# Gated delta rule: the inverse kept on the other half of the partitions, and copies done by ScalarE

## The chip, the cores and the metric

The kernel runs on one core of one Trainium2 chip. The metric is the device time of one launch in microseconds (us). The kernel before took 1951.79 us (median of 3 runs, 1951.33 to 1960.3).

## What is computed

Two blocks of a network follow each other. The change touches one part of the second: the gated delta rule, over 512 positions, 4 heads of width 128, in both directions. The reference works in chunks of 64 positions:

```python
g = jnp.cumsum(g.reshape(b, h, n, c), axis=-1)
decay = jnp.exp(jnp.where(incl, g[..., :, None] - g[..., None, :], -jnp.inf))
kb = k * beta[..., None]
lower = jnp.where(strict, jnp.einsum('bhnid,bhnjd->bhnij', kb, k) * decay, 0.0)
tmat = lower + jnp.eye(c, dtype=jnp.float32)
rhs = jnp.concatenate([v * beta[..., None], kb * jnp.exp(g)[..., None]], axis=-1)
sol = lax.linalg.triangular_solve(tmat, rhs, left_side=True, lower=True, unit_diagonal=True)
...
def step(state, inp):
    v_new = u_i - jnp.einsum('bhck,bhkv->bhcv', w_i, state)
    o_i = jnp.einsum('bhck,bhkv->bhcv', qg_i, state) + jnp.einsum('bhij,bhjv->bhiv', qk_i, v_new)
    state = state * gl_i[..., None, None] + jnp.einsum('bhck,bhcv->bhkv', kg_i, v_new)
```

The other parts (projections, attention, cross attention, feed-forward, and the whole first block) are the same in both kernels.

## The kernel before

Each engine has its own program, and counting semaphores order them. Nothing plans the order around the change: it is the order in which the loops are written out. The gated delta rule runs in four stages, one after the other; the profile's lines are given in brackets.

**Chunks.** The kernel takes chunks of 128 positions (four, `DN_CHUNKS`), so that the unit-triangular matrix of a chunk is 128x128 for each of 4 heads and 2 directions. For each chunk TensorE (PE) makes decay sums and the products of keys and queries [L2262, `four`], ScalarE (ACT) takes absolute values and exponentials [L1048, L1055, L1056, L1058], VectorE (DVE) builds `dn_lower` [L1553] and the query products [L1556] out of them. PE also turns k and v by token [L2282, L2284], and VectorE copies the turned tiles out of PSUM [L1558, L1559]; PE needs these two banks free for the next chunk (`dn_tok`).

**Inverses.** The inverse of each 128x128 matrix is built from its two 64x64 diagonal blocks. Block 0 lies in partitions 0 to 63, block 1 in 64 to 127 (`HALF`). A group `p` holds 8 matrices, 512 columns; there are 4 groups, and 6 levels, so 24 steps `q = 4 l + p`. A step has two PE calls and two DVE parts:

- `half_products(q)` [L2303]: for 8 matrices and both halves, `dn_lower` times the transposed inverse `dn_inv_t`; 16 products of 64x64.
- `half_masked(q)` [L1574]: DVE multiplies the bank by a mask into `dn_half`. At level 0 it also writes `dn_inv_t` as identity less `dn_half` [L1579], in two instructions, one for each half of the partitions.
- `inverse_products(q)`: from level 1 on, two products for each half, one for `dn_inv_t` [L2324] and one for `dn_inv` [L2327], with 32 moving columns each. At level 0 it turns `dn_half` [L2320].
- `inverse_update(q)`: DVE subtracts both from the inverses [L1593, L1594]; at level 0 it writes `dn_inv` as identity less the turned bank, again in two instructions [L1590].

PE runs `half_products(q)` and then `inverse_products(q - 1)`; DVE runs `half_masked(q)` and then `inverse_update(q - 1)`. Every product of these steps reads partitions of one half and writes PSUM partitions of the same half: it uses the corner (0,0) or (1,1) of the array, where a corner (r,c) is the 64x64 quarter that reads half r and writes half c.

**Corners.** The off-diagonal 64x64 block is made by two more rounds of products [L2343, L2351]. DVE (`corners`) then multiplies the near block by beta [L1605] and the far block by beta [L1606], alternating. Meanwhile GpSimd (POOL) does the same for the other half [L612].

**Recurrence.** Four steps of `v_new`, state and output, in both directions [L2262, L2365, L2385 on PE, L1633, L1639 and others on DVE, L1070 on ACT].

**Small products elsewhere.** The first block also has calls of fp32 products with a 64x64 stationary operand. `scores` [L1892, 32 moving columns] goes in turn through the corners (0,0), (1,0), (0,1), (1,1), and `updates` [L1870, 64 moving columns] through (0,0), (0,1), (1,0), (1,1); in both, what reads half 0 writes one PSUM bank and what reads half 1 another. `carried` [L1917, 64 moving columns] takes only (0,0) and (1,1), into one bank.

A product in fp32 appears in the trace as two records of LDWEIGHTS and two of MATMUL, so a call of 16 products has 32.

Of the kernel before, what the change touches and what calls it, by code (L numbers as in the profile page):

```python
# [22 lines left out]
P = 128  # L23
# [72 lines left out]
def table(entries):  # L96

    at, out = 0, {}
    for name, n in entries:
# [7 lines left out]
CONST2_COLS, N_CONST2 = table([("tri0", P), ("tri1", P), ("inv0", (LEVELS - 1) * HD), ("inv1", (LEVELS - 1) * HD),  # L107
                               ("window", 3 * P), ("rot_half", P), ("inv_freq", 1)])
PAR_COLS, N_PAR = table([("c", 2 * KT), ("norm_g", DEPTH * KT), ("b_mod", DEPTH * N_MOD), ("conv_w", DEPTH * 6),
# [33 lines left out]
def build(nc, tokens, mem, positions, weights, const_d, const2_d, par_d, out):  # L143
    with ExitStack() as ctx:
# [260 lines left out]
        def q_grow(d, c):  # L405
# [52 lines left out]
        dn_grown, dn_qg, dn_qk_ready = sem("dn_grown"), sem("dn_qg"), sem("dn_qk_ready")  # L458
        dn_y_ps, dn_y, dn_z_ps, dn_t = (sem(n) for n in ("dn_y_ps", "dn_y", "dn_z_ps", "dn_t"))
        dn_p_ps, dn_p, dn_c_ps, dn_c, dn_r = (sem(n) for n in ("dn_p_ps", "dn_p", "dn_c_ps", "dn_c", "dn_r"))  # L460
        dn_ks_ps, dn_rhs_ready, dn_v_ps, dn_v, dn_v_end, dn_s_ps, dn_s, dn_o_ps, dn_o = (
# [165 lines left out]
        def _(act):  # L627
# [500 lines left out]
        def _(dve):  # L1128
# [415 lines left out]
            def lower_and_products(n, c):  # L1544

                for d in range(2):
# [9 lines left out]
                    dve.tensor_tensor(dn_qk(u), kq, e, ALU.mult).then_inc(dn_x, 1)  # L1556
                dve.wait_ge(dn_tok_ps, n + 1)
                dve.tensor_copy(k_tok_2(c), by_head(dn_bank(6)))  # L1558
                dve.tensor_copy(v_tok_2(c), by_head(dn_bank(7))).then_inc(dn_tok, 1)  # L1559

            ident_8 = [cst["ident"][rows, rows].unsqueeze(1).broadcast_to([HD, 8, HD]) for rows in HALF]

            def half_masked(q):
# [8 lines left out]
                if 2 <= q < 6:  # L1572
                    dve.wait_ge(dn_t, q - 1)
                dve.tensor_tensor(to_8(dn_half(p)), to_8(dn_bank(p % 2)), mask, ALU.mult).then_inc(dn_y, 1)  # L1574
                if l == 0:
                    dve.wait_ge(dn_y, q + 1)
                    dve.wait_ge(dn_qg, DN_GROWN[NLAT - 1])
                    for r, rows in enumerate(HALF):
                        dve.tensor_tensor(to_8(dn_inv_t(p))[rows], ident_8[r], to_8(dn_half(p))[rows], ALU.subtract)  # L1579

            def inverse_update(q):

                l, p = divmod(q, 4)
                d = p % 2
                side = 1 - d
                dve.wait_ge(dn_z_ps, q + 1)
                if l == 0:
                    to_8 = lambda v: v.rearrange("p (n t) -> p n t", t=HD)
                    for r, rows in enumerate(HALF):
                        ins = dve.tensor_tensor(to_8(dn_inv(p))[rows], ident_8[r], to_8(dn_bank(4 + p % 2))[rows], ALU.subtract)  # L1590
                else:
                    mine, other_side = (lambda v: halves(v, 1 << l)[:, :, side, :]), (lambda v: halves(v, 1 << l)[:, :, 1 - side, :])
                    dve.tensor_tensor(mine(dn_inv_t(p)), mine(dn_inv_t(p)), mine(dn_bank(2 + p % 2)), ALU.subtract)  # L1593
                    ins = dve.tensor_tensor(other_side(dn_inv(p)), other_side(dn_inv(p)), other_side(dn_bank(4 + p % 2)), ALU.subtract)  # L1594
                ins.then_inc(dn_t, 1)

            def corners(n):

                dve.wait_ge(dn_c_ps, n + 1)
                for s in (2 * n, 2 * n + 1):  # L1600
                    for d in range(2):
                        u, c = dn_unit(d, s), chunk_at(d, s)
                        lo, to = HALF[0], HALF[d]
                        factor = beta[:, c, 4 * d:4 * d + 4].unsqueeze(2).broadcast_to([P, 4, HD])
                        dve.tensor_tensor(dn_lower(u)[lo, :, lo], by_head2(dn_inv_t(u // 2), s)[lo], factor[lo], ALU.mult)  # L1605
                        dve.tensor_tensor(dn_lower(u)[to, :, HALF[1 - d]], by_head2(dn_bank(n), s)[to], factor[to], ALU.mult).then_inc(dn_c, 1)  # L1606
# [103 lines left out]
        def _(pe):  # L1710
# [576 lines left out]
            def half_products(q):  # L2287
# [7 lines left out]
                else:  # L2295
                    pe.wait_ge(dn_t, q - 3)
                if q >= 2:
                    pe.wait_ge(dn_y, q - 1)
                for m in range(8):
                    for rows in HALF:  # L2300
                        x = dn_lower(2 * p + m // 4)[rows, m % 4, rows]
                        inv_t = dn_inv_t(p)[rows, HD * m:HD * m + HD] if l else cst["ident"][rows, rows]
                        last = pe.matmul(dn_bank(p % 2)[rows, HD * m:HD * m + HD], x, inv_t, start=True, stop=True, skip_group_check=True)  # L2303
                last.then_inc(dn_y_ps, 1)

            def inverse_products(q):
# [7 lines left out]
                if q >= 2:  # L2314
                    pe.wait_ge(dn_t, q - 1)
                for m in range(8):
                    at = slice(HD * m, HD * m + HD)
                    if l == 0:
                        for rows in HALF:
                            last = pe.matmul(dn_bank(4 + p % 2)[rows, at], dn_half(p)[rows, at], cst["ident"][rows, rows], start=True,  # L2320
                                             stop=True, skip_group_check=True)
                        continue
                    for rows in HALF:
                        pe.matmul(halves(dn_bank(2 + p % 2)[rows, at], 1 << l)[:, :, side, :], dn_inv(p)[rows, at],  # L2324
                                  halves(dn_half(p)[rows, at], 1 << l)[:, :, side, :], start=True, stop=True, skip_group_check=True)
# [12 lines left out]
            for n in range(2):  # L2338
                pe.wait_ge(dn_t, steps - 2 + 2 * n)
                for m in range(8):  # L2340
                    for d in range(2):
                        frm, to, p = HALF[1 - d], HALF[d], 2 * n + d
                        last = pe.matmul(dn_bank(6 + n)[to, HD * m:HD * m + HD], dn_lower(2 * p + m // 4)[frm, m % 4, to],  # L2343
                                         dn_inv_t(p)[frm, HD * m:HD * m + HD], start=True, stop=True, skip_group_check=True)
                last.then_inc(dn_p_ps, 1)
            for n in range(2):
                pe.wait_ge(dn_p, n + 1)
                for m in range(8):
                    for d in range(2):
                        to, p = HALF[d], 2 * n + d  # L2350
                        last = pe.matmul(dn_bank(n)[to, HD * m:HD * m + HD], dn_inv(p)[to, HD * m:HD * m + HD],  # L2351
                                         dn_corner(n)[to, HD * m:HD * m + HD], start=True, stop=True, skip_group_check=True)
                last.then_inc(dn_c_ps, 1)
# [183 lines left out]
def constants():  # L2537
# [16 lines left out]
                        + [np.where(t >= s, 0, NEG), np.zeros((P, P)), np.where(t <= s, 0, NEG), rotation(halves),  # L2554
                           np.tile(inv_freq, 4)[:, None]], 1)
    assert c1.shape[1] == N_CONST and c2.shape[1] == N_CONST2
# [75 lines left out]
```

## Time and profile before

| | us |
|---|---|
| timed runs, median (lowest, highest) | 1951.79 (1951.33, 1960.3) |
| the profiled execution, its own time | 1953.26 |
| its span in the trace | 1951.5 |
| PE busy | 1766.4 (91%) |
| DVE busy | 812.1 (42%) |
| ACT busy | 717.0 (37%) |
| POOL busy | 598.2 (31%) |

The profiled execution ran 1.5 us longer than the median of the timed runs, and its span is 1.8 us shorter than its own time. All durations below come from this one execution. The gated delta rule from the first chunk to the last output is the stretch from about 1195 to 1343 us of the span. The share of PE says little there: PE's rows count as busy from the start of a record to its modelled end, and small products overlap each other. What tells how fast a call of small products goes is the distance from its first start to the first start of the next call, divided by the records in it.

### The profile page before, as it was taken

To read this page: it belongs to the slowest core of one execution; us is meant where nothing else is said; L and a number is where in the kernel's file an instruction comes from. 1 tells how busy PE (TensorE), PEld (TensorE's weight loads), DVE (VectorE), ACT (ScalarE), POOL (GpSimd) and SP (SyncE) were. 2 spreads that over 40 slices of the span, in tenths; PEclk is the share of its full clock that TensorE was granted. 3 is DMA by queue.
4 is the path that set the end of the run, shared out by engine and by line. 5 is a ranking of instruction groups with operands and counts; after the bars stand their busy time and mean duration, and the time that the engine had idled before them with its cause. 6 is when DMAs were issued, how large, how long until landed. Compare 5 with 4: busy or idle time off the path is not lost.

```text
span 1951.5 us, 32357 instructions
## 1 busy us (share of the span) xinstructions
PE 1766.4 (91%) x13594; PEld 1405.0 (72%) x13594; DVE 812.1 (42%) x1471; ACT 717.0 (37%) x1115; POOL 598.2 (31%) x318
## 2 busy tenths in 40 slices
PE   6799899978989988989879988888999999999996
PEld 2687788845878766657767766887678678888885
DVE  0301165417350265355656658656424443323112
ACT  3323413226343624254543877003433432222222
POOL 0221312173113323453013411311334334444442
PEclk9899999999999999999899999899999999999998
DMA  8344311130122111311422210000220222222231
GB/s 324 103 158 142 108 35 45 62 113 1 45 86 86 65 56 55 109 44 65 140 99 86 86 55 2 3 3 12 76 76 22 76 76 91 93 98 97 97 107 66
DMA packets 43145, 154.27 MB, mean 79 GB/s; under 512 B 4480, under 2 KB 5632, under 8 KB 42752
## 3 DMA queue, kind: packets, MB, share of 16 engines
q1 hardware_dynamic: 39456, 142.82, 21.2%
q10 hardware_dynamic: 3552, 9.44, 1.3%
q8 instruction: 108, 1.77, 0.4%
q14 instruction: 29, 0.24, 0.0%
HBM read 148.05 MB, written 4.19 MB: 78 GB/s over the span
## 4 chain that ended last, share of the span: by engine, by line
PE 41%; DVE 7%; ACT 2%; issue 2%; DVEq 0%; ACTq 0%
PE wide_ps L1751 29%; PE wide_ps L1772 2%; PE pair_ps L2327 1%; PE wide_ps L2324 1%; PE wide_ps L2303 1%; PE wide_ps L2262 1%; DVE xn L1519 1%; PE duo_ps L2431 1%; PE wide_ps L2412 1%; DVE xn L1669 1%; PE wide_ps L1787 1%; PE pair_ps L1826 1%; DVE ring_r L1170 1%; PE pair_ps L2262 0%; DVE h L1673 0%
## 5 line engine op out<-in xcount | busy, mean ns | idle before, releaser
L528 POOL TENSOR_TENSOR ring_r<-ring,scratch_r 128x1024 fp32r<-128x1024 f32 x179 | 432.2, 2415 | 1082.8 <-ACT scratch_r L700 1054.8
L1751 PE MATMUL wide_ps<-xn_r,scratch_r 128*128 128x512 f32 (+1 forms) x1320 | 490.1, 371 | 0.0
L1751 PE MATMUL wide_ps<-work_r,scratch_r 128*128 128x512 f32 (+1 forms) x1151 | 445.2, 387 | 22.9 <-DVE xn_r L1162 12.0
L700 ACT ACTIVATE scratch_r<-ring 128x1024 fp32r<-128x1024 f32 x195 | 206.7, 1061 | 609.7 <-PE wide_ps L1751 456.8
L1751 PE MATMUL wide_ps<-work_r,ring_r 128*128 128x512 f32 (+1 forms) x1151 | 429.5, 373 | 0.0
L1751 PEld LDWEIGHTS wide_ps<-xn_r,scratch_r 128*128 128x128 f32 x1320 | 252.1, 191 | 49.1 <-issue 5.4
L1751 PEld LDWEIGHTS wide_ps<-work_r,scratch_r 128*128 128x128 f32 x1151 | 218.7, 190 | 75.0 <-issue 18.8
L1751 PEld LDWEIGHTS wide_ps<-work_r,ring_r 128*128 128x128 f32 x1151 | 218.8, 190 | 40.0
L1751 PE MATMUL wide_ps<-proj_r,scratch_r 128*128 128x512 f32 x704 | 238.0, 386 | 1.5 <-DVE proj_r L1162 1.5
L1751 PEld LDWEIGHTS wide_ps<-proj_r,scratch_r 128*128 128x128 f32 x704 | 133.1, 189 | 31.1 <-DVE proj_r L1162 1.9
L687 ACT ACTIVATE proj<-wide_ps 128x512 f32<-128x512 f32 (+2 forms) x116 | 73.8, 636 | 163.8 <-PE wide_ps L1751 154.8
L1267 DVE SCALAR_TENSOR_TENSOR proj<-proj,par_sb,qe 128x768 f32<-128x768 f32 (+1 forms) x6 | 6.2, 1037 | 213.2 <-ACT qe L651 213.2
L1315 DVE TENSOR_TENSOR work<-work 128x512 f32<-128x512 f32 (+2 forms) x35 | 36.4, 1041 | 125.0 <-ACT work L659 124.2
L1751 PE MATMUL wide_ps<-proj_r,ring_r 128*128 128x512 f32 x208 | 82.6, 397 | 0.0
L1751 PE MATMUL wide_ps<-conv_tmp_r,scratch_r 128*128 128x512 f32 (+1 forms) x185 | 69.4, 375 | 0.0
L1751 PE MATMUL wide_ps<-conv_tmp_r,ring_r 128*128 128x512 f32 (+1 forms) x185 | 69.2, 374 | 0.0
L1703 DVE TENSOR_TENSOR proj<-proj,qe 128x512 f32<-128x512 f32 x11 | 27.5, 2501 | 82.2 <-ACT qe L687 82.2
L1703 DVE TENSOR_TENSOR proj<-proj,state 128x512 f32<-128x512 f32 x11 | 27.5, 2500 | 80.5 <-ACT state L687 80.5
L1335 DVE TENSOR_TENSOR h<-h,work 128x768 f32<-128x768 f32 (+1 forms) x16 | 29.8, 1862 | 65.3 <-ACT work L871 65.3
L659 ACT ACTIVATE work<-h 128x512 f32<-128x512 f32 (+2 forms) x56 | 36.2, 660 | 54.2 <-DVE work L1315 16.6
L1751 PEld LDWEIGHTS wide_ps<-proj_r,ring_r 128*128 128x128 f32 x208 | 39.3, 189 | 9.3
L2016 PE MATMUL wide_ps<-proj 64*128 64x256 f32 (+1 forms) x144 | 29.7, 529 | 17.1 <-ACT xn L827 14.5
(392 smaller groups left out, 2906.4 us busy)
## 6 DMA issues: line engine op xcount, KB each, us to landing
ring<-weights SPq DMA_DIRECT2D x260, 512.0 KB, 3.5
h<-tokens SPq DMA_DIRECT2D x4, 768.0 KB, 11.8
h<-tokens ACTq DMA_DIRECT2D x1, 3072.0 KB, 10.0
out<-h ACTq DMA_DIRECT2D x1, 2048.0 KB, 7.3
h<-out ACTq DMA_DIRECT2D x1, 2048.0 KB, 8.6
out<-h SPq DMA_DIRECT2D x8, 256.0 KB, 2.1
const_sb<-const SPq DMA_DIRECT2D x1, 1089.0 KB, 6.3
h<-mem ACTq DMA_DIRECT2D x1, 1024.0 KB, 12.1
```

The source lines that it names most:

```text
L528: pool.tensor_tensor(as_r(wt), wt, as_r(w_lead(m)).bitcast(F32), ALU.subtract).then_inc(w_split, 1)
L659: act.activation(square_sum(n)[:, 0:w] if first else squares(n)[:, k % 2, 0:w], src, ACT.Square).then_inc(sq_ready, 1)
L687: act.activation(dst, wide_ps[0:rows, g % 2 if bank is None else bank, 0:w], func).then_inc(evacuated, 1)
L700: act.activation(as_r(w_lead(m)), ring[:, c % RING, :], ACT.Copy).then_inc(w_lead_ready, 1)
L1170: dve.tensor_tensor(as_r(wt), wt, as_r(w_lead(m)).bitcast(F32), ALU.subtract).then_inc(w_split, 1)
L1315: dve.tensor_tensor(total, total, squares(n)[:, k % 2, 0:w], ALU.add).then_inc(sq_used, 2 if k == 1 else 1)
L1335: dve.tensor_tensor(h[:, n, 0:w], h[:, n, 0:w], resid[:, n % 2, 0:w], ALU.add).then_inc(h_ready, 1)
L1519: link(dve.tensor_tensor_reduce(probs(n)[:, r * (b - a):(r + 1) * (b - a)], win_bank(n, r)[:, 0:b - a], cst2["window"][:, ma:mb], HD ** -0 ...
L1703: dve.tensor_tensor(tile_2[:, t, :], tile_2[:, t, :], up_2[t % 2], ALU.mult).then_inc(ffn_ready, 1)
L1751: last = pe.matmul(wide_ps[:, bank, a:b], wt[:, cols], as_r(x[:, a:b]), start=n == 0 and p == 0, stop=n == len(k_order) - 1 and p == 2)
L1772: last = pe.matmul(ps[:, a:b], wt[:, cols], as_r(x[:, a:b]), start=k == 0 and p == 0, stop=k == KT - 1 and p == 2)
L2016: last = pe.matmul(wide_ps[:, r, a:b], proj[rows, AQ + i, c * CH:(c + 1) * CH], proj[rows, AK, a:b], start=True, stop=True)
```

## The change

The inverse `dn_inv` now lies on the other half of the partitions: that of block 0 in partitions 64 to 127, that of block 1 in 0 to 63, while `dn_inv_t` stays. From level 1 on `half_products` writes the other half, and so does the first product of `inverse_products`; its second product stays on its own half. At level 0 `dn_inv` comes from turning `dn_inv_t` instead of `dn_half`, so that it is a plain copy, which ScalarE does (semaphore `dn_t0`), and `dn_inv_t` is written by one instruction with a new constant `idents` (two stacked 64x64 identities). ScalarE also takes over the two copies of turned k and v. VectorE multiplies the eight near blocks (`near_corners`) before it waits for the far ones.

```diff
+        def inverse_done(engine, q):
+            engine.wait_ge(*((dn_t0, q) if q <= 4 else (dn_t, q - 4)))
...
 # ScalarE, at the end of each chunk, and after the four chunks
+                act.wait_ge(dn_tok_ps, n + 1)
+                act.activation(k_tok_2(c), by_head(dn_bank(6)), ACT.Copy)
+                act.activation(v_tok_2(c), by_head(dn_bank(7)), ACT.Copy).then_inc(dn_tok, 1)
+            for q in range(4):
+                act.wait_ge(dn_z_ps, q + 1)
+                act.activation(dn_inv(q), dn_bank(4 + q % 2), ACT.Copy).then_inc(dn_t0, 1)
...
 # VectorE, half_masked
-                dve.tensor_tensor(to_8(dn_half(p)), to_8(dn_bank(p % 2)), mask, ALU.mult).then_inc(dn_y, 1)
+                masked = dve.tensor_tensor(to_8(dn_half(p)), to_8(dn_bank(p % 2)), mask, ALU.mult)
                 if l == 0:
-                    dve.wait_ge(dn_y, q + 1)
+                    link(masked)
                     dve.wait_ge(dn_qg, DN_GROWN[NLAT - 1])
-                    for r, rows in enumerate(HALF):
-                        dve.tensor_tensor(to_8(dn_inv_t(p))[rows], ident_8[r], to_8(dn_half(p))[rows], ALU.subtract)
+                    masked = dve.tensor_tensor(to_8(dn_inv_t(p)), idents_8, to_8(dn_half(p)), ALU.subtract)
+                masked.then_inc(dn_y, 1)
 # VectorE, inverse_update: the branch for l == 0 goes, and the loop
-                if q:
+                if q > 4:
                     inverse_update(q - 1)
+            dve.wait_ge(dn_t, steps - 4)
+            for n in range(2):
+                near_corners(n)
             for n in range(2):
                 corners(n)
...
 # TensorE, half_products
-                    pe.wait_ge(dn_t, q - 3)
+                    inverse_done(pe, q - 3)
...
+                        to = HALF[1 - r] if l else rows
-                        last = pe.matmul(dn_bank(p % 2)[rows, HD * m:HD * m + HD], x, inv_t, ...)
+                        last = pe.matmul(dn_bank(p % 2)[to, HD * m:HD * m + HD], x, inv_t, ...)
 # TensorE, inverse_products, level 0
-                            last = pe.matmul(dn_bank(4 + p % 2)[rows, at], dn_half(p)[rows, at], cst["ident"][rows, rows], ...)
+                            last = pe.matmul(dn_bank(4 + p % 2)[HALF[1 - r], at], dn_inv_t(p)[rows, at], cst["ident"][rows, rows], ...)
 # and the levels above; the second product is as before
-                        pe.matmul(halves(dn_bank(2 + p % 2)[rows, at], 1 << l)[:, :, side, :], dn_inv(p)[rows, at],
+                        pe.matmul(halves(dn_bank(2 + p % 2)[HALF[1 - r], at], 1 << l)[:, :, side, :], dn_inv(p)[rows, at],
                                   halves(dn_half(p)[rows, at], 1 << l)[:, :, side, :], ...)
```

VectorE, from the last chunk to the first steps of level 1, stood like this (L1558 and L1559 are the copies, `proj<-wide_ps,proj` the mask, L1579 and L1590 the level 0 parts):

```order
L1553 SCALAR_TENSOR_TENSOR xn<-wide_ps,small,xn 128x128 x4
L1555 COPY small<-xn 128x4
L1556 TENSOR_TENSOR work<-pair_ps,xn 128x512
L1558 COPY proj<-duo_ps 128x512
L1559 COPY proj<-duo_ps 128x4x128
L1574 TENSOR_TENSOR proj<-wide_ps,proj 128x512
L1579 TENSOR_TENSOR work<-const_sb,proj 64x512 x2
L1574 TENSOR_TENSOR proj<-wide_ps,proj 128x512
L1579 TENSOR_TENSOR work<-const_sb,proj 64x512 x2
L1590 TENSOR_TENSOR xn<-const_sb,pair_ps 64x512 x2
L1574 TENSOR_TENSOR proj<-wide_ps,proj 128x512
```

and now (L1582 is the mask, L1586 the identity less it):

```order
L1564 SCALAR_TENSOR_TENSOR xn<-wide_ps,small,xn 128x128 x4
L1566 COPY small<-xn 128x4
L1567 TENSOR_TENSOR work<-pair_ps,xn 128x512
L1582 TENSOR_TENSOR proj<-wide_ps,proj 128x512
L1586 TENSOR_TENSOR work<-proj 128x512
L1582 TENSOR_TENSOR proj<-wide_ps,proj 128x512
L1586 TENSOR_TENSOR work<-proj 128x512
L1582 TENSOR_TENSOR proj<-wide_ps,proj 128x512
```

The copies and the parts of `inverse_update` at level 0 are gone from this queue, and L1579's pairs have become single instructions.

ScalarE, for the last chunk and up to the recurrence (L1048 is the absolute value, L1055 to L1058 the exponentials, L1061 the copy between the two corner rounds, L1070 the recurrence), stood like this:

```order
L1048 ACTIVATE xn<-wide_ps,small 128x128 x4
L1055 ACTIVATE work<-wide_ps 128x512
L1056 ACTIVATE small<-wide_ps 128x4
L1058 ACTIVATE xn<-xn 128x512
L1061 ACTIVATE proj<-duo_ps 128x512 x2
L1070 ACTIVATE xn<-wide_ps 128x512 x8
```

and now (L1053 to L1063 as above, L1065 and L1066 the copies of k and v, L1069 those of the inverses):

```order
L1053 ACTIVATE xn<-wide_ps,small 128x128 x4
L1060 ACTIVATE work<-wide_ps 128x512
L1061 ACTIVATE small<-wide_ps 128x4
L1063 ACTIVATE xn<-xn 128x512
L1065 ACTIVATE proj<-duo_ps 128x512
L1066 ACTIVATE proj<-duo_ps 128x4x128
L1069 ACTIVATE xn<-pair_ps 128x512 x4
L1072 ACTIVATE proj<-duo_ps 128x512 x2
```

Three rows were added: two copies at the end of each of the four chunks, behind the exponentials of the second direction and ahead of the next chunk's absolute values, and four copies of the inverses after the last chunk.

## Rows read from the trace of the kernel before

**Rows 1.** The page: the span and the busy shares.
```profile
span 1951.5 us, 32357 instructions
PE 1766.4 (91%) x13594; PEld 1405.0 (72%) x13594; DVE 812.1 (42%) x1471; ACT 717.0 (37%) x1115; POOL 598.2 (31%) x318
```

**Rows 2.** Chain of work, 1215 to 1312 us: start, us, what.
```profile
1220.56 0.60 DVE proj L1558
1221.16 0.60 DVE proj L1559
1221.75 0.61 DVE proj L1574
...
1239.90 0.70 DVE proj L1574
...
1254.20 0.96 PE wide_ps L2303 x32
...
1257.00 0.96 PE wide_ps L2303 x32
```

**Rows 3.** Groups by line, 1170 to 1320: busy us, mean ns, idle before and its releaser.
```profile
L1574 DVE TENSOR_TENSOR proj<-wide_ps,proj 128x512 f32<-128x512 f32 x24 | 16.6, 693 | 5.7 <-PE wide_ps L2303 5.1
...
L1579 DVE TENSOR_TENSOR work<-const_sb,proj 64x512 f32<-64x512 f32 x8 | 10.7, 1334 | 0.2
...
L1048 ACT ACTIVATE xn<-wide_ps,small 128x128 f32<-128x128 f32 x32 | 9.2, 386 | 3.8 <-PE wide_ps L2262 3.8
...
L1590 DVE TENSOR_TENSOR xn<-const_sb,pair_ps 64x512 f32<-64x512 f32 x8 | 5.5, 685 | 0.1
...
L1605 DVE TENSOR_TENSOR xn<-work,small 64x256 f32<-64x256 f32 x8 | 4.8, 596 | 2.1 <-PE wide_ps L2351 2.0
...
L1606 DVE TENSOR_TENSOR xn<-wide_ps,small 64x256 f32<-64x256 f32 x8 | 3.4, 421 | 0.1
...
L1061 ACT ACTIVATE proj<-duo_ps 128x512 f32<-128x512 f32 x2 | 1.2, 598 | 81.9 <-PE duo_ps L2343 81.9
```

**Rows 4.** PE in order of time, loop and corners: start, us, line, shape, count.
```profile
1251.23 1.13 PE L2303 MATMUL wide_ps<-work,xn 64*64 64x64 f32 x32
1254.03 1.13 PE L2303 MATMUL wide_ps<-work,xn 64*64 64x64 f32 x32
...
1293.23 1.13 PE L2303 MATMUL wide_ps<-work,xn 64*64 64x64 f32 x32
1294.19 0.26 PE L2324 MATMUL wide_ps<-proj,xn 64*64 64x32 f32 x4
```

**Rows 5.** PE in order of time, other places with 64x64 products (first block).
```profile
248.14 0.90 PE L1892 MATMUL wide_ps<-h,proj 64*64 64x32 f32 x48
248.86 0.88 PE L1892 MATMUL pair_ps<-h,proj 64*64 64x32 f32 x48
...
293.20 0.93 PE L1870 MATMUL duo_ps<-h 64*64 64x64 f32 x48
293.95 0.88 PE L1870 MATMUL wide_ps<-h 64*64 64x64 f32 x48
...
303.30 1.50 PE L1917 MATMUL pair_ps<-h,state 64*64 64x64 f32 x44
304.63 1.45 PE L1917 MATMUL pair_ps<-h,qe 64*64 64x64 f32 x44
```

**Rows 6.** ACT in order of time, the first and last parts of the four chunks.
```profile
1198.39 1.14 ACT L1048 ACTIVATE xn<-wide_ps,small 128x128 f32<-128x128 f32 x4 [1.00 <-PE wide_ps L2262]
...
1208.72 1.14 ACT L1048 ACTIVATE xn<-wide_ps,small 128x128 f32<-128x128 f32 x4 [1.97 <-PE wide_ps L2262]
...
1216.90 0.72 ACT L1058 ACTIVATE xn<-xn 128x512 f32<-128x512 f32 x1
```

**Rows 7.** Stretches: us, busy PE, PEld, DVE, ACT, POOL; granted clock, DMA share, GB/s.
```profile
1221.00:1224.00 3.00, 2.35 (x57) 2.22 (x54) 2.96 (x4) 0.00 (x0) 3.00 (x4) 0.72 0.02 5
...
1236.00:1240.00 4.00, 3.57 (x64) 3.43 (x64) 3.79 (x6) 0.00 (x0) 3.42 (x3) 0.58 0.01 4
...
1244.00:1248.00 4.00, 4.00 (x80) 4.00 (x79) 0.99 (x2) 0.00 (x0) 0.00 (x0) 0.50 0.01 4
...
1260.00:1298.00 38.00, 38.00 (x1317) 38.00 (x1314) 19.40 (x41) 0.00 (x0) 0.00 (x0) 1.00 0.02 4
```

**Rows 8.** DVE in order of time, from the last update to the recurrence.
```profile
1298.45 0.41 DVE L1594 TENSOR_TENSOR xn<-xn,pair_ps 128x256 f32<-128x256 f32 x1
...
1300.88 0.42 DVE L1605 TENSOR_TENSOR xn<-work,small 64x256 f32<-64x256 f32 x1 [2.01 <-PE wide_ps L2351]
...
1308.86 1.29 DVE L1633 TENSOR_TENSOR xn<-wide_ps,small 128x512 f32<-128x512 f32 x2
```

**Rows 9.** PE in order of time, the first and a later step of the recurrence.
```profile
1309.61 2.07 PE L2262 MATMUL pair_ps<-xn,scratch 128*128 128x128 f32 x8 [5.54 <-DVE xn L1633]
...
1315.59 1.95 PE L2262 MATMUL wide_ps<-scratch,proj 128*128 128x128 f32 x16
...
1321.00 1.16 PE L2262 MATMUL pair_ps<-xn,scratch 128*128 128x128 f32 x8
...
1324.68 1.95 PE L2262 MATMUL wide_ps<-scratch,proj 128*128 128x128 f32 x16
```

More of the change, by code:

```diff
@@ L107 @@
 CONST2_COLS, N_CONST2 = table([("tri0", P), ("tri1", P), ("inv0", (LEVELS - 1) * HD), ("inv1", (LEVELS - 1) * HD),
-                               ("window", 3 * P), ("rot_half", P), ("inv_freq", 1)])
+                               ("window", 3 * P), ("rot_half", P), ("inv_freq", 1), ("idents", HD)])
 PAR_COLS, N_PAR = table([("c", 2 * KT), ("norm_g", DEPTH * KT), ("b_mod", DEPTH * N_MOD), ("conv_w", DEPTH * 6),
@@ L459, in build @@
         dn_y_ps, dn_y, dn_z_ps, dn_t = (sem(n) for n in ("dn_y_ps", "dn_y", "dn_z_ps", "dn_t"))
+        dn_t0 = sem("dn_t0")
         dn_p_ps, dn_p, dn_c_ps, dn_c, dn_r = (sem(n) for n in ("dn_p_ps", "dn_p", "dn_c_ps", "dn_c", "dn_r"))
@@ L1556, in lower_and_products @@
                     dve.tensor_tensor(dn_qk(u), kq, e, ALU.mult).then_inc(dn_x, 1)
[L1557 to L1561, printed above, removed]
+            idents_8 = cst2["idents"].unsqueeze(1).broadcast_to([P, 8, HD])
             def half_masked(q):
@@ L1572, in half_masked @@
                 if 2 <= q < 6:
-                    dve.wait_ge(dn_t, q - 1)
-                dve.tensor_tensor(to_8(dn_half(p)), to_8(dn_bank(p % 2)), mask, ALU.mult).then_inc(dn_y, 1)
+                    dve.wait_ge(dn_y, q - 1)
+                masked = dve.tensor_tensor(to_8(dn_half(p)), to_8(dn_bank(p % 2)), mask, ALU.mult)
                 if l == 0:
-                    dve.wait_ge(dn_y, q + 1)
+                    link(masked)
                     dve.wait_ge(dn_qg, DN_GROWN[NLAT - 1])
-                    for r, rows in enumerate(HALF):
-                        dve.tensor_tensor(to_8(dn_inv_t(p))[rows], ident_8[r], to_8(dn_half(p))[rows], ALU.subtract)
+                    masked = dve.tensor_tensor(to_8(dn_inv_t(p)), idents_8, to_8(dn_half(p)), ALU.subtract)
+                masked.then_inc(dn_y, 1)
             def inverse_update(q):
@@ L1586, in inverse_update, with near_corners @@
                 dve.wait_ge(dn_z_ps, q + 1)
[L1587 to L1595, printed above, removed]
+                mine, other_side = (lambda v: halves(v, 1 << l)[:, :, side, :]), (lambda v: halves(v, 1 << l)[:, :, 1 - side, :])
+                dve.tensor_tensor(mine(dn_inv_t(p)), mine(dn_inv_t(p)), mine(dn_bank(2 + p % 2)), ALU.subtract)
+                dve.tensor_tensor(other_side(dn_inv(p)), other_side(dn_inv(p)), other_side(dn_bank(4 + p % 2)),
+                                  ALU.subtract).then_inc(dn_t, 1)
+            def near_corners(n):
+                for s in (2 * n, 2 * n + 1):
+                    for d in range(2):
+                        u, lo = dn_unit(d, s), HALF[0]
+                        factor = beta[:, chunk_at(d, s), 4 * d:4 * d + 4].unsqueeze(2).broadcast_to([P, 4, HD])
+                        dve.tensor_tensor(dn_lower(u)[lo, :, lo], by_head2(dn_inv_t(u // 2), s)[lo], factor[lo], ALU.mult)
             def corners(n):
@@ L2299, in half_products @@
                 for m in range(8):
-                    for rows in HALF:
+                    for r, rows in enumerate(HALF):
                         x = dn_lower(2 * p + m // 4)[rows, m % 4, rows]
                         inv_t = dn_inv_t(p)[rows, HD * m:HD * m + HD] if l else cst["ident"][rows, rows]
-                        last = pe.matmul(dn_bank(p % 2)[rows, HD * m:HD * m + HD], x, inv_t, start=True, stop=True, skip_group_check=True)
+                        to = HALF[1 - r] if l else rows
+                        last = pe.matmul(dn_bank(p % 2)[to, HD * m:HD * m + HD], x, inv_t, start=True, stop=True, skip_group_check=True)
                 last.then_inc(dn_y_ps, 1)
@@ L2314, in inverse_products @@
                 if q >= 2:
-                    pe.wait_ge(dn_t, q - 1)
+                    inverse_done(pe, q - 1)
                 for m in range(8):
@@ L2318, in inverse_products @@
                     if l == 0:
-                        for rows in HALF:
-                            last = pe.matmul(dn_bank(4 + p % 2)[rows, at], dn_half(p)[rows, at], cst["ident"][rows, rows], start=True,
+                        for r, rows in enumerate(HALF):
+                            last = pe.matmul(dn_bank(4 + p % 2)[HALF[1 - r], at], dn_inv_t(p)[rows, at], cst["ident"][rows, rows], start=True,
                                              stop=True, skip_group_check=True)
                         continue
-                    for rows in HALF:
-                        pe.matmul(halves(dn_bank(2 + p % 2)[rows, at], 1 << l)[:, :, side, :], dn_inv(p)[rows, at],
+                    for r, rows in enumerate(HALF):
+                        pe.matmul(halves(dn_bank(2 + p % 2)[HALF[1 - r], at], 1 << l)[:, :, side, :], dn_inv(p)[rows, at],
                                   halves(dn_half(p)[rows, at], 1 << l)[:, :, side, :], start=True, stop=True, skip_group_check=True)
@@ L2338, in _ @@
             for n in range(2):
-                pe.wait_ge(dn_t, steps - 2 + 2 * n)
+                inverse_done(pe, steps - 2 + 2 * n)
                 for m in range(8):
@@ L2342, in _ @@
                         frm, to, p = HALF[1 - d], HALF[d], 2 * n + d
-                        last = pe.matmul(dn_bank(6 + n)[to, HD * m:HD * m + HD], dn_lower(2 * p + m // 4)[frm, m % 4, to],
+                        last = pe.matmul(dn_bank(6 + n)[frm, HD * m:HD * m + HD], dn_lower(2 * p + m // 4)[frm, m % 4, to],
                                          dn_inv_t(p)[frm, HD * m:HD * m + HD], start=True, stop=True, skip_group_check=True)
@@ L2349, in _ @@
                     for d in range(2):
-                        to, p = HALF[d], 2 * n + d
-                        last = pe.matmul(dn_bank(n)[to, HD * m:HD * m + HD], dn_inv(p)[to, HD * m:HD * m + HD],
-                                         dn_corner(n)[to, HD * m:HD * m + HD], start=True, stop=True, skip_group_check=True)
+                        frm, to, p = HALF[1 - d], HALF[d], 2 * n + d
+                        last = pe.matmul(dn_bank(n)[to, HD * m:HD * m + HD], dn_inv(p)[frm, HD * m:HD * m + HD],
+                                         dn_corner(n)[frm, HD * m:HD * m + HD], start=True, stop=True, skip_group_check=True)
                 last.then_inc(dn_c_ps, 1)
@@ L2554, in constants @@
                         + [np.where(t >= s, 0, NEG), np.zeros((P, P)), np.where(t <= s, 0, NEG), rotation(halves),
[L2555 removed]
+                           np.tile(inv_freq, 4)[:, None], np.tile(np.eye(HD), (2, 1))], 1)
     assert c1.shape[1] == N_CONST and c2.shape[1] == N_CONST2
```

3 lines of the change are left out of this document (1 added, 2 removed).

## The prediction, written before the changed kernel ran

> **What bounds the kernel now.** The page first: PE is busy for 91% of the span, which says that the end is set by PE over most of the kernel, but not what it does between 1195 and 1343 us [rows 1]. The chain of waits over that stretch shows two regimes. From 1221.75, where the first mask starts, to 1239.90, where the fifth starts (level 0), the chain is VectorE's own queue, instruction behind instruction [rows 2]. From there to 1298.86, the end of the last update [rows 8], it is PE: the calls of `half_products` follow each other every 2.80 us, and PE is busy without a gap [rows 2, 4, 7]. Behind the last update the chain is VectorE's again: it waits 2.01 us, works through 16 small multiplications and reaches the recurrence at 1308.86 [rows 8]. PE waits 5.54 us for that [rows 9]. So 87 us between the first mask and the recurrence are bound by the instructions that the change edits. DMA's share there is 0.01 to 0.02, and I see no transfer or weight preparation that uses these 87 us as cover [rows 7].
>
> **The loop from level 1 on (the large term).** A step has 32 records of `half_products` and 64 of `inverse_products`. From 1293.23 to 1294.19 the first take 0.96 us, 30 ns each; the other 1.84 us of a 2.80 us step are 28.75 ns for each of the 64 [rows 4]. The first stream 64 columns and the second 32, and yet the distance is the same, so streaming does not set it. What both share is that two corners work in turn: one corner gets a record every 57 to 60 ns. Other calls tell what four corners do: L1892, also with 32 moving columns, issues 48 records in 0.72 us, 15.0 ns each, and L1870, with 64, 48 in 0.75 us, 15.6 ns; L1917, with two corners, 44 in 1.33 us, 30.2 ns [rows 5]. In all five calls a corner gets a record every 57 to 62 ns, and the distance is that over the number of corners. After the change `inverse_products` goes through (0,1), (1,0), (0,0), (1,1) and should take 64 x 15.0 ns = 0.96 us in place of 1.84. `half_products` changes corners but still has two of them, so it stays at 0.96. A step becomes 1.92 us, and 20 steps gain 20 x 0.88 = 17.6 us. Can VectorE follow? Its step is a mask of 0.69 us and two subtractions, 1.5 us in all; its busy share is 19.40 of 38 us for 2.80 us steps, 1.43 us a step [rows 3, 7]. The mask lies beside PE's next call, and 0.4 us a step remain: PE stays the bound, with little to spare. Bounds: nothing (28.75 ns stays) to 17.6; I take 17.6, since L1892 is nearest in shape. What differs is that there each half read had its own bank, while here both halves read write one bank, in two corners.
>
> The Trainium skill, TensorEngine Tiling (Array Packing), Restrictions and Gotchas, speaks against this: different row tiles are not to access the same PSUM bank at the same time. Here the trace disagrees for the two corners in use: L2303 reads both halves into one bank at 30 ns a record, as fast as a pair can be that is not held up [rows 4, 5].
>
> **Level 0.** Between the masks at 1221.75 and 1239.90, 18.15 us, VectorE runs four masks (2.8 us), eight L1579 of 1.334 us (10.7) and six of the L1590 of 0.685 us (4.1), 17.6 in all [rows 2, 3]. Afterwards each of the four steps has a mask of 0.69 and one subtraction over 128 partitions. It is not in the trace; nearest is L1579, with the same 512 columns for each partition and both operands in SBUF, and half the partitions change nothing in the columns. So 1.33, with 0.69 (L1574) below and 2.67 above, if against that the time went by partitions. Four steps are 4 x (0.69 + 1.33 + 0.07 for the wait) = 8.4 us, a gain of 9.8. PE's part is 4 x 2 calls of 0.96, 7.7 us at full clock, and lies beside it. Now `dn_y` comes only after the subtraction, and PE's next but one half product and the turning call wait behind it; with 0.96 us calls that fits into the 2.1 us step. The four ScalarE copies (0.60 each, L1061) lie beside VectorE: the first is wanted four calls later. Bounds: if the granted clock is at its lower level, as it was in parts (0.72 at 1221, 0.58 at 1236) [rows 7], PE needs up to 3.8 us for a step, and the gain falls to 3; at 2.67 it falls to 4.4; at 0.69 it is PE's 7.7 that counts, gain 10.5.
>
> **Chunks.** VectorE loses two copies for each chunk; those behind the last one go from the chain: the first mask starts at 1220.56 in place of 1221.75, 1.2 us earlier [rows 2]. But ScalarE takes them into its queue ahead of the next chunk's absolute values. It now spans 19.2 us (1198.39 to 1217.62) with 3.8 - 1.0 = 2.8 us idle inside, so 16.4 of work [rows 3, 6]; six copies ahead of the last exponential add 3.6: it ends at 1218.4, 0.8 later than now, and the last `lower_and_products` behind it by as much. Gain 0.4. PE's next turning waits for the copies (`dn_tok`), and they for PE's turning: if these waits do not interlock as smoothly, ScalarE loses up to 0.6 more in each of three chunks. Bounds: loss of 1.5 to gain of 1.2.
>
> **Corners.** From 1298.86 to 1308.86 are 10.0 us. Afterwards the eight L1605 (0.596 each, 4.8) fill the wait, then eight L1606 at 0.42 (3.4): 8.2 us, gain 1.8 [rows 3, 8]. The far products come 3.0 us behind the last update and are no bound. Without GpSimd's disturbance an L1605 is 0.42 like L1606: bounds 0.5 to 3.4.
>
> **Clock behind it.** PE sat idle for 5.54 us before 1309.61, and the first recurrence step, up to L2262's 16, took 5.98 us where a later one took 3.68 [rows 9]. With near blocks done early PE's wait splits into about 2.7 and 1.4 us. The clock may stay up: 0 to 2.3, I take 1.2. In the loop the clock stood at 0.50 at 1244 [rows 7]: the 58.96 us from the fifth mask on are 1.9 more than PE's calls make at full clock, 20 x 1.84 + 20 x 0.96 and 1.1 for the last update = 57.1. I leave that loss in (0 to 1.9 to be gained).
>
> **Sum.** 17.6 + 9.8 + 0.4 + 1.8 + 1.2 = 30.8 us. Against the profiled execution's 1953.26 that is 1922.5; it was 1.5 above the median of 1951.79, and against the median 1921.0. The constant `idents` adds 32 KB to a transfer long before and costs nothing.
>
> **Rivals.**
> First, the corners do not overlap beyond two, because a bank takes records from only one half read at a time or the order of the four does not suit: 28.75 ns stays. Against it rows 5, for it only that no call there mixes halves within a bank. Gain 13.2, time 1938.6. Chance 0.05.
>
> Second, the four corners overlap only in part, because the sequencer starts records no closer than some distance below 28.75 ns. Halfway to 15.0 it is 21.9: the loop gains 1280 x 6.9 ns = 8.8, in all 22.0, time 1929.8. L1892's and L1870's distances speak against any floor above 15.6 ns. Chance 0.05.
> The Trainium skill, TensorE: Matmul & The Clock Gate, Back-to-back issue gap, states such a floor, about 25 ns from start to start for 1 to 64 columns. By it, as an estimate, the loop would gain 1280 x 3.75 ns = 4.8 and the time be 1933.8. The trace disagrees, with 15.0 ns at L1892 [rows 5].
>
> Third, slower: the corners (0,1) and (1,1), and (1,0) and (0,0), write the same PSUM partitions, in banks 2 or 3 and 4 or 5 of which each is now fed from both halves. If each record has to wait for the other's write, the distance doubles to 57.5 ns: the loop loses 1280 x 28.75 ns = 36.8 us, less 13.2 of the rest: 23.6 slower, 1975.4. It turns the sign above 39 ns a record (13.2 us / 1280 + 28.75). L1892 and L1870 write the same partitions from two corners without this. Chance 0.03.
>
> The forecast itself has 0.87.
>
> **How the numbers follow.** The forecast's own range: all terms at their good ends 17.6 + 10.5 + 1.2 + 3.4 + 2.3 + 1.9 = 36.9, 1915; at the poor ends 17.6 + 3 - 1.5 + 0.5 = 19.6, 1932. Both ends at once are unlikely; I give 1914 to 1934, which holds nearly all of the forecast and the second rival too, with about 0.85 inside. About 0.5% (9.8 us) is what a measurement of this kernel tells from no change. Faster by more: the forecast, the second rival and two thirds of the first, 0.94; within: 0.04; slower: 0.02 of the third.
>
> **What would show it.** PE's calls of the level 1 loop every 1.92 us, and 64 records of `inverse_products` in about 0.96; VectorE's level 0 in four pairs of about 2.1 us, in all 8.4 to 10; ScalarE's last exponential of the chunks at about 1218.4; the eight far multiplications without the near ones between them, and the recurrence about 8.2 us behind the last update. It is wrong if the distance stays above 20 ns, if VectorE's masks start later than the half products end, or if PE runs level 0 at half clock.

## The result, and the profile after

The changed kernel took 1935.75 us (median of 6 runs, 1933.37 to 1943.84), the kernel before 1953.28 (6 runs, 1949.05 to 1960.58): a ratio of 0.9909 with a 95% interval of 0.9881 to 0.9937. It is faster by 17.5 us; the prediction had 30.8 us less and a time of 1921, with 1914 to 1934 as its range. The sign is right, the size is not.

The page of the changed kernel has the same number of PE records, and a span shorter by 17.3 us [rows 1]:

```profile
span 1934.2 us, 32349 instructions
PE 1746.2 (90%) x13594; PEld 1382.4 (71%) x13594; DVE 795.1 (41%) x1451; ACT 723.2 (37%) x1127; POOL 597.4 (31%) x318
```

The stages below run from ScalarE's first absolute value, the first mask, the fifth mask, the end of the last update, the first instruction of the recurrence on VectorE, and the first squares behind it. Each number is a difference of two times in a trace, in us.

| stage | predicted gain | before | after | gain |
|---|---|---|---|---|
| chunks | 0.4 | 23.29 | 21.70 | 1.6 |
| level 0 | 9.8 | 18.22 | 10.46 | 7.8 |
| levels 1 to 5 | 17.6 | 58.97 | 54.78 | 4.2 |
| corners | 1.8 | 9.99 | 7.18 | 2.8 |
| recurrence | 1.2 | 33.04 | 30.73 | 2.3 |
| the rest, to the end | 0 | 609.58 | 611.23 | -1.7 |

The last row is no effect of the change: over nine traces with the same code there, it lies between 609.4 and 611.8. Most of what is missing is in levels 1 to 5. The groups of that loop in the changed kernel, by line, for 1215 to 1293 us (busy us, mean ns, then the idle time of PE just before and its releaser; L2317 is `half_products`, L2338 and L2341 the two products):

```profile
L2341 PE MATMUL pair_ps<-xn,proj 64*64 64x32 f32 x640 | 24.8, 222 | 5.4 <-issue 5.3
L2338 PE MATMUL wide_ps<-proj,xn 64*64 64x32 f32 x640 | 24.2, 219 | 3.8 <-issue 3.8
L2317 PE MATMUL wide_ps<-work,xn 64*64 64x64 f32 x640 | 24.0, 220 | 4.2 <-issue 4.2
```

PE now stands idle for 13.4 us of the loop, and for 13.3 of them the releaser is "issue": nothing that the profile shows held it, no semaphore of VectorE or ScalarE. In order of time (start, us, line, count, idle before):

```profile
1240.23 0.81 PE L2317 MATMUL wide_ps<-work,xn 64*64 64x64 f32 x20
1242.06 0.51 PE L2317 MATMUL wide_ps<-work,xn 64*64 64x64 f32 x11 [1.03 <-issue]
1242.36 0.25 PE L2341 MATMUL pair_ps<-xn,proj 64*64 64x32 f32 x2
...
1243.31 0.25 PE L2317 MATMUL wide_ps<-work,xn 64*64 64x64 f32 x1
...
1245.51 0.24 PE L2338 MATMUL wide_ps<-proj,xn 64*64 64x32 f32 x1 [0.75 <-issue]
```

Two things are to be seen. From 1242.36 to 1243.31 all 64 records of `inverse_products` go in 0.95 us, where they took 1.84 [rows 4]: the four corners overlap as foreseen. And the stop before 1242.06 falls into the middle of a call, where no instruction waits for anything. The DMA view for 1236 to 1244 shows in its 40 slices of 0.2 us what goes on beside it:

```profile
DMA  0000000000000000300000000000000000003000
...
q8 instruction: 2, 0.03, 1.7%
```

The only transfers are two packets of the queue named "instruction", 16 KB each, at about 1239.2 and 1243.2. Each comes before a stop's end. It is so along the whole loop: the 13 stops there last 0.6 to 1.3 us each, each ends 2.2 to 2.7 us behind the start of a packet, and the next packet starts 1.1 to 1.6 us behind the stop's end. Over the whole page this queue has 108 packets and 1.77 MB. PE has 13594 pairs of LDWEIGHTS and MATMUL; that is 65 bytes for each of the 27188 and 126 pairs for each packet. So I take these packets to be PE's program, about 128 pairs in each with a few other instructions among them; the runs below bear it out, since the page's 108 packets fall to 105 where 320 pairs are left out, and to 99 and 96 where a loop saves three and four passes over 384 pairs. Over 1236 to 1284 there are 13 of them, one in 3.7 us:

```profile
q8 instruction: 13, 0.21, 1.9%
```

### The profile page after: what moved, and what is told of

Read it like the earlier page. It is cut to its first block, busy times and chain, and to the rows that moved or that the text cites. A ratio compares the mean times of both kernels' runs of the same rounds, so it can differ in the third digit from the quotient of the medians.

```text
span 1934.2 us, 32349 instructions
## 1 busy us (share of the span) xinstructions
PE 1746.2 (90%) x13594; PEld 1382.4 (71%) x13594; DVE 795.1 (41%) x1451; ACT 723.2 (37%) x1127; POOL 597.4 (31%) x318
## 3 DMA queue, kind: packets, MB, share of 16 engines
q8 instruction: 108, 1.77, 0.4%
## 4 chain that ended last, share of the span: by engine, by line
PE 41%; DVE 5%; ACT 3%; issue 2%; DVEq 0%; ACTq 0%
PE wide_ps L1764 29%; PE wide_ps L1785 2%; PE wide_ps L2317 1%; PE pair_ps L1839 1%; DVE xn L1530 1%; PE duo_ps L2445 1%; PE wide_ps L2426 1%; PE pair_ps L2341 1%; PE wide_ps L2275 1%; PE wide_ps L1800 1%; DVE ring_r L1181 1%; PE wide_ps L2338 0%; ACT xn L1053 0%; DVE xn L1682 0%; PE duo_ps L2399 0%
```

## The experiments

Theory A is formed on this: the supply of PE's instructions bounds the loop, a block of 128 record pairs in about 3.7 us (the expectations were written with 3.6). Theory B is the rival that the profile cannot exclude by itself: the stops are a wait for another engine, and the corners are worth what was predicted.

**Two corners** (`two_corners`) undoes the corners alone.

```diff
-                        to = HALF[1 - r] if l else rows
+                        to = rows
...
-                        pe.matmul(halves(dn_bank(2 + p % 2)[HALF[1 - r], at], 1 << l)[:, :, side, :], dn_inv(p)[rows, at],
+                        pe.matmul(halves(dn_bank(2 + p % 2)[rows, at], 1 << l)[:, :, side, :], dn_inv(p)[rows, at],
```

The turning at level 0 and the two corner rounds go back with it.

> The changed kernel with only the corners undone: the inverse lies on its own half again and every product of the loop reads and writes the same half; the copies by ScalarE, the single instruction at level 0 and the early near blocks stay. Theory A (the supply of PE's instructions bounds the loop: a block of 16 KB, which is 128 records of LDWEIGHTS and 128 of MATMUL, comes no faster than about every 3.6 us): a step takes 2.80 us of array time, 3.73 us a block, so PE's stops vanish and the loop is only 2 to 4 us longer than in the changed kernel; time 1936 + 2 to 4 = 1938 to 1940. Theory B (what the prediction said: the corners are worth 17.6 us, and the stops have a cause of their own that stays, such as a wait for VectorE): 1946 to 1953.

Measured: 1939.21 us (6 runs, 1936.55 to 1943.6), ratio to the kernel before 0.9926 (0.9911 to 0.9941). Levels 1 to 5 took 56.73 us, and PE's groups show no idle time in them:

```profile
L2341 PE MATMUL pair_ps<-xn,proj 64*64 64x32 f32 x640 | 38.3, 219 | 0.0
L2338 PE MATMUL wide_ps<-proj,xn 64*64 64x32 f32 x640 | 37.8, 217 | 0.0
...
L2317 PE MATMUL wide_ps<-work,xn 64*64 64x64 f32 x640 | 22.5, 220 | 0.0
```

The time is what theory A foresaw, and B's 1946 to 1953 did not come. 15 us are gained against the kernel before without any corner. The intervals of this kernel and the changed one overlap (0.9926 and 0.9909), so what the corners are worth in the changed kernel is not settled by the times; levels 1 to 5 of its one trace are 1.9 us shorter than here.

Here and below the kernel before had 1954.32 us as its median in the same runs, for the last three experiments 1953.91.

**Fewer records** (`fewer`) leaves out the second product for four of eight matrices (`for rows in HALF if m % 2 else ():`), so its inverses are not the right ones.

> The changed kernel, with the second product of inverse_products left out for every other of the 8 matrices (levels 1 to 5), so the inverses are wrong; 320 of the loop's 1920 records go, all waits stay. Theory A: time goes with the records, 320 x 3.6 us / 128 = 9.0 us less than the changed kernel, 1927; stops of about 1.2 us come still once in 128 records, that is every 1.6 steps. Theory B (stops from a wait for another engine, once or twice a step): at most the array's 320 x 15 ns = 4.8 us go, and if VectorE is late nothing: 1931 to 1936, and the stops keep their place within a step.

Measured: 1932.03 us (4 runs, 1922.76 to 1933.77), ratio 0.9866 (0.9842 to 0.989). Levels 1 to 5 took 47.97 us, 6.8 less than in the changed kernel: more than B's 4.8, less than A's 9.0. PE's idle time by "issue" fell from 13.3 to 7.4 us:

```profile
L2317 PE MATMUL wide_ps<-work,xn 64*64 64x64 f32 x640 | 23.9, 220 | 2.8 <-issue 2.8
L2338 PE MATMUL wide_ps<-proj,xn 64*64 64x32 f32 x640 | 23.2, 218 | 2.0 <-issue 2.0
...
L2341 PE MATMUL pair_ps<-xn,proj 64*64 64x32 f32 x320 | 19.8, 229 | 2.6 <-issue 2.6
```

The time lies in B's range of 1931 to 1936 and 5 us above A's 1927, with runs too far apart to tell much. The stops speak for A: the eleven from 1242.57 to 1280.90 us are 3.83 us apart on average, which is 1.6 steps of 2.40 us, as A said, where B wanted them at a fixed place of each step. But they lasted 0.3 to 0.9 us and not 1.2, and a block took 3.8 us and not 3.6, so the supply is no fixed time for a block. The run leans to A and does not settle the size.

**A loop on PE** (`loop`) asks the question directly: instructions that do not have to be fetched again. For it the products compute all 64 columns of a block, so that the code is the same at every level.

```diff
-            for q in range(steps + 1):
-                if q < steps:
-                    half_products(q)
-                if q:
-                    inverse_products(q - 1)
+            for q in range(5):
+                both(q)
+            with pe.Fori(0, LEVELS - 3) as turn:
+                for q in range(5, 9):
+                    both(q, turn * 4)
+            for q in range(steps - 3, steps + 1):
+                both(q)
```

Here `both(q, more)` is the two calls, with `more` added to what their waits count to; the ScalarE copies of the inverses count in `dn_t` too, and each call within the loop first counts up a semaphore that nobody waits for (`pe_tick`).

> The changed kernel with levels 1 to 4 of the inverses on PE as a hardware loop of 4 turns over one body of 4 steps (768 instructions, 48 KB). For that the products of inverse_products compute all 64 columns of a block, of which VectorE uses the same 32 as before, and the waits count with the turn. Theory A, if the sequencer keeps 48 KB: turns 2 to 4 run without stops, 12 steps x (2.7 - 1.95) = 9 us less than the changed kernel, 1927. Theory A, if each block is fetched again: the stops stay, and each of 3 jumps back adds a fetch of its own that nothing covers, up to 3.6 us: 1936 to 1947. Theory B: the stops stay whatever the code's place, and the jumps add some tenths: 1936 to 1938.

Measured: 1924.78 us (5 runs, 1922.53 to 1930.75), ratio 0.9849 (0.9831 to 0.9867). Levels 1 to 5 took 43.69 us, 11.1 less than in the changed kernel. That is theory A in its first form, in which the engine keeps the 48 KB, and by 2 us more than the 1927 expected. From 1242 to 1267 no packet of any queue starts in the trace, and PE is busy for 24.22 of 25 us:

```profile
1242.00:1267.00 25.00, 24.22 (x1221) 23.88 (x1212) 18.26 (x39) 0.00 (x0) 0.00 (x0) 1.00 0.00 0
```

What is left of the stops stands at the jumps back, three of 0.25 to 0.28 us. Two of them:

```profile
1243.04 1.09 PE L2321 MATMUL wide_ps<-work,xn 64*64 64x64 f32 x30 [0.28 <-issue]
...
1258.90 1.09 PE L2321 MATMUL wide_ps<-work,xn 64*64 64x64 f32 x30 [0.25 <-issue]
```

They are two turns apart, 7.93 us for a turn: three steps of 1.87 to 1.89 us and one of 2.31 with the jump in it.

**All columns without the loop** (`full_columns`) is its control.

> Control for the loop: the changed kernel with 64 moving columns in place of 32 in both products of inverse_products, of which VectorE uses the same 32; no loop. Theory A: same instructions, same blocks; 64 records take 1.0 us in place of 0.93, all inside the stops: same time as the changed kernel within 1 us. If instead the columns counted (two passes of 64 in four corners, 14 ns a record), the same; only if they did not overlap would it be 15 us or more longer.

Measured once: 1939.07 us; levels 1 to 5 took 55.63 us. The stops are there, 14.1 us of them by "issue", so the loop's gain is not from the columns:

```profile
L2341 PE MATMUL pair_ps<-xn,proj 64*64 64x64 f32 x640 | 25.4, 222 | 5.6 <-issue 5.5
L2338 PE MATMUL wide_ps<-proj,xn 64*64 64x64 f32 x640 | 24.8, 219 | 4.4 <-issue 4.4
L2317 PE MATMUL wide_ps<-work,xn 64*64 64x64 f32 x640 | 23.6, 218 | 4.2 <-issue 4.2
```

One run leaves the last microseconds open.

**The loop with two corners** (`loop_two`) takes the supply away as a bound and asks what the corners are worth then.

> The hardware loop on PE, with two corners in place of four (the inverse on its own half). Theory A: the code is held in the loop, so the supply bounds neither this nor the four-corner loop, and the corners are worth what the prediction gave them: in the loop 0.9 us for each of its 16 steps, 14 us, and some 2 in the steps outside: from the fifth mask to the last update 56.7 us as in two_corners (which had no stops to lose) against 43.7 in the loop with four corners; time 1938. Rival: the loop helps for another reason than the code (its waits are placed otherwise, or the 64 columns): then loop_two is faster than two_corners by about the same 10 us, 1928.

Measured: 1938.2 us (6 runs), ratio 0.9922 (0.9906 to 0.9938). Levels 1 to 5 took 57.20 us, 0.5 us longer than without the loop (56.73). So neither the loop nor what was added to write it gains by itself. The loop gives nothing where two corners are the bound, and the corners give at most 2 us where the supply is; between `loop_two` and `loop` they are worth 13.5 us of the stage and 13.4 of the time. Both bounds lay almost on top of each other in the kernel before: 3.73 us for 128 record pairs by two corners, and 3.7 by the supply. The same 29 us, 1243 to 1272, tell it in one row each; the x behind PE's busy time counts its records. First the changed kernel:

```profile
1243.00:1272.00 29.00, 20.72 (x998) 19.82 (x992) 14.81 (x31) 0.00 (x0) 0.00 (x0) 1.00 0.02 5
```

Then two corners without the loop:

```profile
1243.00:1272.00 29.00, 29.00 (x1002) 29.00 (x999) 15.26 (x32) 0.00 (x0) 0.00 (x0) 1.00 0.02 5
```

Two corners in the loop:

```profile
1243.00:1272.00 29.00, 29.00 (x993) 28.95 (x989) 14.46 (x30) 0.00 (x0) 0.00 (x0) 1.00 0.00 0
```

And four corners in the loop over all levels, of the next experiment:

```profile
1243.00:1272.00 29.00, 28.26 (x1432) 27.93 (x1431) 21.08 (x44) 0.00 (x0) 0.00 (x0) 1.00 0.00 0
```

The changed kernel runs 998 records in this stretch and two corners 1002: four corners only turned busy time into idle time. With both bounds gone it is 1432.

**All five levels in the loop** (`loop_all`): `pe.Fori(0, LEVELS - 2)`, and nothing behind it.

> The loop with all 20 steps from level 1 on, 5 turns; PE makes one call of half_products too many at the end (0.93 us), into a bank that nobody reads. Theory A: the four steps behind the loop, which ran at 2.7 us with stops, run at 1.9: 3.2 us less, less 0.9 for the extra call: 1922 to 1924 against 1924.8 for the loop of 4 turns. Rival (what comes behind the loop has to be fetched anyway, and its wait only moves into the corner rounds): 1925 to 1926.

Measured: 1924.7 us (5 runs, 1922.03 to 1927.69), ratio 0.9848 (0.9829 to 0.9867). Levels 1 to 5 took 42.58 us, 1.1 less than with four turns and not 2.3: behind the four turns stood two stops, of 0.48 and 1.08 us, where 3.2 us had been put down. The time lies between theory A's range and the rival's; the corner stage took 7.6 us in both loops, so no wait of the rival's kind shows there. The timed runs do not tell the two kernels apart. It beats both kernels: 29 us below the one before, 11 below the changed one.

**Copies back on VectorE** (`copies_back`): the changed kernel with the two copies of k and v in `lower_and_products` again.

> The changed kernel with the copies of k and v by token back on VectorE. From ScalarE's first absolute value to the first mask it took 21.7 us in the changed kernel and 23.3 before. If the copies are what made the difference: 23.3 again, all other stages as in the changed kernel. If it came from elsewhere (the granted clock, where the trace begins): 21.7.

Measured once: 1938.42 us. The first stage took 23.28 us, to 0.01 us what it took before; with the copies on ScalarE seven traces have 21.66 to 21.70, so the copies made the whole of that term. Levels 1 to 5 took 56.73 us with the same code as the changed kernel's 54.78: in a loop bound by supply the stage varies by 2 us from execution to execution (one trace of each), which is why single runs and stage times do not settle the last microseconds here.

## Why the prediction was wrong, step by step

**The loop from level 1 on** is the step that failed. The prediction said "A step becomes 1.92 us, and 20 steps gain 20 x 0.88 = 17.6 us". The term of 17.6 us measured 4.2, and of these 2.2 came without the corners (58.97 to 56.73 us with two corners, the clock's, see below); the corners themselves gave 0 to 2 us by the three traces with stops and all records, 54.78 (the changed kernel), 55.63 (`full_columns`) and 56.73 us (`copies_back`). Its measure of the corners was right: 64 records took 0.95 us against 0.96 foreseen, a step without a stop 1.87 against 1.92, and with the code held in a loop the same corners gave 13.5 us over the stage. Wrong was the sentence "PE stays the bound": it asked only VectorE whether it could follow. The sentence that no transfer mattered here passed over the 4 GB/s of rows 7: in the kernel before, all packets between 1251 and 1298 us, 13 of them, are of the instruction queue. The step's 96 record pairs are three quarters of a block, and at one block of 128 pairs in 3.7 us they take 2.8 us, however fast the corners are. The kernel before used up a block in 128 / 96 x 2.80 = 3.73 us and so hid this bound almost exactly under its own; rows 5 came from calls of 88 to 96 records between large products, shorter than a block, and could not show it. By 54.78 / 1920 a record pair took 28.5 ns on average, where the prediction had 20. Why a block takes 3.7 us, though its packet is moved in about 1, no run here shows; the order in the trace (a stop ends, 1.1 to 1.6 us later the next packet starts, 2.2 to 2.7 us after that the next stop ends) suggests that the next block is asked for only when the one before it begins to be used.

The Trainium skill, Runtime: NRT & Kernel Launch, Instruction fetch mechanics, says that the sequencer fetches its program in blocks of 16 KiB through a DMA queue of its own, and that crossing a block costs one DMA tail-bump, mostly hidden. The trace agrees on the block and the queue. On "mostly hidden" it disagrees for dense small products: 0.6 to 1.3 us a block stay. The same section gives PE 128 KiB for instructions, and a few lines further on only two blocks with no benefit from locality; the loop of 48 KB, three blocks, that ran for 25 us without a packet agrees with the first and not with the second.

**The rivals.** The first, with 1938.6 us, lay nearer than the forecast, but by luck: it had the corners not overlapping, and they do. The second (1929.8, and the estimate of 1933.8 beside it, which lay nearest of all) had a floor on the distance from start to start; the records go at 15 ns, and what holds them up is a mean over a block, so that nearness is luck too. The third did not come. No rival had the supply of instructions as its bound. (By its own parts the chance of a clear gain adds up to 0.95, not 0.94.)

**Level 0** gave 7.8 instead of 9.8. Its four steps took 10.46 us, not 8.4. VectorE stood waiting for PE's half products, for 1.74 and for 0.51 us; the longer wait:

```profile
1225.68 0.69 DVE L1582 TENSOR_TENSOR proj<-wide_ps,proj 128x512 f32<-128x512 f32 x1 [1.74 <-PE wide_ps L2317]
```

The sum was made for full clock, and the prediction named half clock as its bound. The windows (us, busy PE, PEld, DVE, ACT, POOL, then the granted clock) show it at its lower level over the first half:

```profile
1219.00:1222.00 3.00, 1.97 (x32) 1.78 (x32) 2.97 (x4) 0.00 (x0) 3.00 (x4) 0.50 0.03 5
1222.00:1226.00 4.00, 3.68 (x91) 3.68 (x93) 2.23 (x4) 0.60 (x1) 4.00 (x3) 0.56 0.00 0
1226.00:1230.00 4.00, 3.01 (x109) 2.87 (x107) 3.69 (x4) 1.19 (x2) 4.00 (x4) 1.00 0.03 6
```

PE had stood still for 2.10 us before 1219.94. That the clock made the waits is argued from this; no run had level 0 at full clock, and all eight traces since have 10.4 to 10.6 us. The subtraction itself was sized well:

```profile
L1586 DVE TENSOR_TENSOR work<-proj 128x512 f32<-128x512 f32 x4 | 5.5, 1375 | 0.1
```

1.375 us against 1.33 taken from L1579 [rows 3]. Both are means of unlike ones: two of the four took 1.04 us and two about 1.7, and the eight of L1579 0.93 to 1.78. So twice the partitions cost little or nothing.

**Chunks** gave 1.6 instead of 0.4. ScalarE's copies lay on its queue and its 2.8 us of idle time went, both as foreseen, but one behind the other the copies cost 0.48 to 0.49 us and not the 0.598 of a lone one [rows 3]. Its last exponential ended 19.05 us behind its first absolute value, where 20.0 had been worked out. The chain of the changed kernel, start and us:

```profile
1202.02 0.49 ACT scratch L1065
1202.51 0.49 ACT proj L1066
```

**Corners** gave 2.8 instead of 1.8, since the near blocks one behind the other took 3.6 us where 4.8 had been taken (here L1606 has the near blocks and L1616 the far ones):

```profile
L1606 DVE TENSOR_TENSOR xn<-work,small 64x256 f32<-64x256 f32 x8 | 3.6, 515 | 0.0
L1616 DVE TENSOR_TENSOR xn<-wide_ps,small 64x256 f32<-64x256 f32 x8 | 3.4, 421 | 0.2
```

**The clock behind it** was right in kind: PE's wait before the recurrence was 1.56 us instead of 5.54 [rows 9], and the stage took 30.73 us in all eight traces since, against 33.04. The granted clock was at its lower level (0.50) for 6.7 us in the kernel before, from just ahead of it, and at 1.00 all through it now. Before:

```profile
1307.70:1314.40 6.70, 4.79 (x22) 4.79 (x23) 3.79 (x7) 1.19 (x2) 0.00 (x0) 0.50 0.01 2
```

In the changed kernel:

```profile
1292.20:1323.00 30.80, 29.22 (x256) 28.87 (x256) 21.43 (x56) 4.82 (x9) 2.28 (x5) 1.00 0.01 1
```

The whole 2.3 us came, where 1.2 had been put down. The 1.9 us of the loop came too: 56.73 us with two corners, where 57.1 had been worked out for full clock, against 58.97.

The first product of the recurrence in the changed kernel:

```profile
1292.98 1.16 PE L2275 MATMUL pair_ps<-xn,scratch 128*128 128x128 f32 x8 [1.56 <-DVE xn L1646]
```

Without the loop's term the sum was 13.2, and two corners measured 15.1 less than the kernel before (1954.32 to 1939.21), the loop's 2.2 us of clock among them.

## What to carry to other kernels

Before an engine is made faster, count what its instructions themselves need: here a TensorE program streamed one record pair in 28.5 to 30 ns over a long stretch, which is as fast as two corners go, so that dense 64x64 products in fp32 gained little or nothing from four corners, however well these overlapped in a short burst. Signs of it are idle time by "issue" in the middle of a call, once in 128 pairs, with a packet of the instruction queue ahead of it. Code that repeats can be a hardware loop on that engine, if its access patterns are made alike; here it paid in columns that nobody reads and still gained 11 us.

## What the runs showed of the hardware that was not expected

- PE's program comes in packets of 16 KB, one in 3.7 to 3.8 us while PE waits for it; the packet itself is moved in 0.9 to 1.4 us.
- A hardware loop on PE over 384 pairs of load and product, three packets' worth or 48 KB, ran its turns behind the first without any fetch: no packet on any queue for 25 us and more, and PE busy for 97% of it; a jump back left PE idle for about 0.25 us. The page's total fell from 108 packets to 99 with four turns and to 96 with five.
- At the upper level of the granted clock each corner of the array took a record pair in about 60 ns in every fp32 case seen, so two corners gave 28.75 to 30 ns from start to start and four gave 15, for 32 and for 64 moving columns alike, and also with both halves reading into one PSUM bank.
